# A hybrid decoder step on one core: both halves of every cache page fetched by SyncE, none by GpSimd

## The reference

```python
# cache (DEPTH, N_PHYS, 128, 4, 2, 64): slots k_cmp, v_cmp, k_sel, v_sel; 32 pages per sample
past = cache[layer, page_table, :, :2]                  # every page: compressed keys and values
k_c = _compress(cmp_rows[:, :, 0], w1[0], b1[0], w2[0])
v_c = _compress(cmp_rows[:, :, 1], w1[1], b1[1], w2[1])
o_cmp, imp = _nsa_compressed(q, pos, k_c, v_c)          # imp: weight of each compressed block
idx = _nsa_select(imp, pos, n_blocks)                   # 16 blocks of 64 keys for each query
o_sel = _nsa_sel_attend(q_rot, pos, kg, vg, kpos)       # keys and values of the chosen blocks
o_win = _window_attend(q_rot, ...)                      # the last 512 keys
```

## Time and profile before

| | before |
|---|---|
| median of 3 runs | 2830.82 us |
| profiled execution | 2831.4 us, of which span 2829.7 us |
| mean granted TensorE clock | 0.826 of full speed |
| PE busy | 2296.4 us (81%) |
| DVE / ACT / POOL busy | 1320.5 / 729.9 / 302.0 us |
| fetches of pages | 512 by SyncE, 512 by GpSimd, 128 KB each |

### The profile page before, as it was taken

How to read it: one execution, slowest core, us unless ns; L and a number is a source line. 1 busy time by engine, 2 the same in 40 slices (tenths; PEclk the granted TensorE clock), 3 DMA queues, 4 the chain that set the end, 5 groups by cost and what they waited for, 6 DMA issues and landing times. The chain is left out here.

```text
span 2829.7 us, 35885 instructions
## 1 busy us (share of the span) xinstructions
PE 2296.4 (81%) x12248; PEld 1709.5 (60%) x12248; DVE 1320.5 (47%) x3072; ACT 729.9 (26%) x1512; POOL 302.0 (11%) x516
## 2 busy tenths in 40 slices
PE   6989567569849999997979894774797599999977
PEld 3544467457638887776344443673675488778853
DVE  1343566535515555554114436664454255555431
ACT  1210011024324434341212100110342244434302
POOL 0000000000033222320000000000000332233100
PEclk9999678657879988885989996786587799988869
DMA  4443010010075555642034430100001655566310
GB/s 144 150 141 102 14 28 1 3 44 1 4 172 148 144 142 134 158 114 72 0 107 161 136 89 18 24 1 20 27 1 35 154 144 145 135 158 159 89 67 34
DMA packets 176236, 242.05 MB, mean 86 GB/s; under 512 B 50406, under 2 KB 133126, under 8 KB 175372
## 3 DMA queue, kind: packets, MB, share of 16 engines
q1 hardware_dynamic: 151468, 172.51, 22.1%
q0 software_dynamic: 24576, 67.14, 9.5%
HBM read 223.17 MB, written 24.97 MB: 88 GB/s over the span
## 5 line engine op out<-in xcount | busy, mean ns | idle before, releaser
L588 PE MATMUL bank<-W,hT 128*128 128x512 f32 (+3 forms) x1152 | 444.1, 539 | 30.8 <-DMA W<-in_w_in 21.5
L1526 POOL DMA_DIRECT2D PC<-in_cache_nsa_kv x256 | 150.9, 590 | 2152.0 <-DVEq L195 1687.0
L588 PEld LDWEIGHTS bank<-W,hT 128*128 128x128 f32 x1152 | 216.0, 193 | 228.7 <-issue 182.6
L1212 PE MATMUL bank<-XT,W 128*128 128x256 f32 (+1 forms) x768 | 266.9, 483 | 0.0
L1194 PE MATMUL bank<-CF,RP 128*128 128x128 f32 x1024 | 153.3, 296 | 80.5 <-DVE RP L1182 79.3
L1201 ACT ACTIVATE XT<-bank 128x512 f32<-128x512 f32 x256 | 140.4, 593 | 209.9 <-PE bank L1194 209.0
L1194 PEld LDWEIGHTS bank<-CF,RP 128*128 128x128 f32 x1024 | 123.8, 154 | 94.7 <-DVE RP L1182 84.0
L1694 PE MATMUL bank<-PB,PS 128*128 128x64 f32 x1024 | 176.9, 348 | 3.5 <-ACT PB L1851 3.5
L1526 POOL DMA_DIRECT2D PS<-in_cache_nsa_kv x256 | 150.9, 590 | 220.8 <-issue 165.7
L1694 PEld LDWEIGHTS bank<-PB,PS 128*128 128x128 f32 x1024 | 172.1, 263 | 3.9 <-ACT PB L1851 3.9
L1212 PEld LDWEIGHTS bank<-XT,W 128*128 128x128 f32 x768 | 139.9, 197 | 50.2 <-issue 36.9
(11 more groups left out here) (376 smaller groups left out, 3674.6 us busy)
## 6 DMA issues: line engine op xcount, KB each, us to landing
PC<-in_cache_nsa_kv SPq DMA_DIRECT2D x256, 128.0 KB, 3.8
PC<-in_cache_nsa_kv POOLq DMA_DIRECT2D x256, 128.0 KB, 3.5
PS<-in_cache_nsa_kv POOLq DMA_DIRECT2D x256, 128.0 KB, 4.2
PS<-in_cache_nsa_kv SPq DMA_DIRECT2D x256, 128.0 KB, 4.4
W<-in_w_in SPq DMA_DIRECT2D x48, 512.0 KB, 4.6
XS<-scratch_conv_p SPq DMA_DIRECT2D x24, 384.0 KB
PW<-in_state_nsa_win SPq DMA_DIRECT2D x16, 512.0 KB, 3.9
Wo<-in_w_out SPq DMA_DIRECT2D x4, 2048.0 KB, 12.0
```

What stands on the lines that cost most here:

```text
L588: return nc.tensor.matmul(bk((c * NTILE + t) % 8)[:, 0:b - a], hT[:, k, t * P:(t + 1) * P], W[:, k // 2, k % 2, 0:b - a], start=(k == 0), ...
L1212: mm = nc_(self.v).tensor.matmul(out, self.v['W1'][:, kv, s, :], seg[:, s], start=(s == 0), stop=(s == SEG // PAIRS - 1))
L1526: e.dma_start(where[side * HD:(side + 1) * HD, slot, :, :], A['cache_nsa_kv'][l, page].rearrange("(p r) a g d -> p r (a g d)", r=PAIRS)[:, ...
```

## The change

SyncE now runs the only copy of the sequence and issues both sides of each tile, side 0 and then side 1, behind one wait. GpSimd issues nothing. Each call of `pages` is made twice, once per side. For PC the eight registers of a side are loaded as before; for PS each side has four registers, so a load fetches the four numbers that the next four tiles use. The opening block also issues both sides from SyncE. The data fetched, the buffers and the semaphores are the same, and so is all code of TensorE, ACT and DVE.

```diff
     def pages(e, side, regs, b, n):
-        e.load(regs, ids[0:1, side, b * GT + n:b * GT + n + 8])
+        e.load(regs, ids[0:1, side, b * GT + n:b * GT + n + len(regs)])
         return [e.snap(r) for r in regs]
     def stream(e, side, b, n):
-        for k, page in enumerate(pages(e, side, REGS[side][0:8], b, n)):
+        for k, page in enumerate(pages(e, side, REGS[0][8 * side:8 * side + 8], b, n)):
             fetch(e, PC, k, side, page, 0, pc_rows[side][k])
...
             e.wait_ge(idl, 32)
-            stream(e, 0, 0, 0)
+            for side in range(2):
+                stream(e, side, 0, 0)
             window(e, 0)
...
-        @block.gpsimd
-        def _(e):
-            e.wait_ge(idl, 32)
-            stream(e, 1, 0, 0)
...
-        def transfers(e, side):
-            r = REGS[side]
+        @block.sync
+        def _(e):
+            r = REGS[0]
             def ahead(q, a, z):
...
-                ids_of = pages(e, side, r[0:8], at_q, n)
+                ids_of = [pages(e, side, r[8 * side:8 * side + 8], at_q, n) for side in range(2)]
                 for i in range(a, z):
                     dve.wait(e, f"R{i}.{q}")
-                    fetch(e, PC, i % SLOTS, side, ids_of[i % SLOTS], 0, pc_rows[side][i % SLOTS])
+                    for side in range(2):
+                        fetch(e, PC, i % SLOTS, side, ids_of[side][i % SLOTS], 0, pc_rows[side][i % SLOTS])
             def selected(b, a):
-                ids_of = pages(e, side, r[8:16], b, a // 8 * 8)
+                ids_of = [pages(e, side, r[16 + 4 * side:20 + 4 * side], b, a) for side in range(2)]
                 for k in range(a, a + 4):
-                    fetch(e, PS, k, side, ids_of[k % 8], 256, sel_rows[side][k // 2])
+                    for side in range(2):
+                        fetch(e, PS, k, side, ids_of[side][k - a], 256, sel_rows[side][k // 2])
```

More of the change, by code:

```diff
@@ L1659, in transfers @@
                 if 0 <= p < last:
-                    if side == 0:
-                        pe.wait(e, f"wpv.{p}")
-                        window(e, p + 1)
+                    pe.wait(e, f"wpv.{p}")
+                    window(e, p + 1)
                 if q + 1 < NB:
@@ L1668, in transfers @@
                         selected(p + 1, 4 * k)
[L1670 to L1676, removed]
         @block.tensor
```

## The result

The change makes the kernel slower: the median goes from 2833.25 us (2829.12 to 2840.72, 4 runs) to 2902.8 us (2898.55 to 2911.35, 4 runs). The ratio is 1.0246, 95% interval 1.0213 to 1.0279. The forecast was 2904.5, a ratio of 1.026. I built the same program twice more (experiments 5 and 10) and it gave 1.0183 (1.0116 to 1.025) and 1.019 (1.0144 to 1.0235).

The account below looks back on a forecast made before the run. TensorE was taken to bound most stretches, the DMA engines pass -1. Terms 8 + 26 + 28 + 12 = 74 us on 2831.4 give 2905, or 2904.5 against the median; forecast 2880 to 2930, 80% range 2866 to 2942.

Parts of the forecast that it names:

- Part 1: Opening block, once per layer: US pieces go out later, behind 16 fetches; 8 us in all (bounds 6 to 14).
- Part 2: Pass -1, once per layer: SyncE's row of 44 fetches and its loads makes tile 13 late; 26 us together.
- The sign that I gave for this stretch: Pass -1 in the new profile: DMA share falls from 0.99 to about 0.75, at 131072 bytes per 0.87 us, 150 GB/s.
- Part 3: Twelve steady passes: SyncE's row from R0 to tile 13 takes 44.6 us, longer than every distance available; 28 us.
- The sign of 1 to 5 us more waiting in each pass: Steady passes in the new profile: TensorE's waits on L1194 grow by 1 to 5 us per pass.
- Part 4: Steady passes: new TensorE waits at tile 13 bring falls of the granted clock, 3.5 to 6.5 us each; 12 us taken.
- a border between 2.35 and 3.25: TensorE waits: a fall of the clock follows every 3.25 us wait, but did not follow one of 2.35 us.
- the longer case: Rival, chance 0.2: the clock falls at each new wait and SyncE's row is longer than summed; 2935 to 2953 us.
- only the fill is paid: Rival, chance 0.2: SyncE keeps up in steady passes; opening and pass -1 costs stay; 2865 to 2877 us.
- it isn't slower: Rival, chance 0.03: SyncE alone issues a fetch per 0.61 us, pass -1 stays rate-bound; 2831 us, give or take 8.

Follow-up runs that it names:

- experiment 1: The changed kernel, but GpSimd again issues side 1 of the PS fetches; 2842.98 us, ratio 1.0028 to the kernel before.
- experiment 9: The changed kernel with every load of page numbers split into loads of one register; 3047.75 us, ratio 1.0727 to the kernel before.
- experiment 2: The changed kernel's sequence, with all page fetches and the window issued by GpSimd instead of SyncE; 2866.55 us, ratio 1.0098 to the kernel before.
- experiment 10: The changed kernel, unedited, built a third time; 2901.36 us, ratio 1.019 to the kernel before.
- Experiment 4: The changed kernel, but in the opening block the window and US pieces are issued ahead of side 1's eight fetches; 2885.22 us, ratio 1.0176.
- experiment 11: The kernel before (two queues), with pass -1 reordered to fetch PC tiles ahead of PS pages, and US pieces issued first in the opening; 2784.28 us, ratio 0.9785.
- experiment 3: The changed kernel with page numbers interleaved so that one load serves both sides, half as many loads; 2882.55 us, ratio 1.0162.

## Why the prediction was right, and where it was not

The time was right to 2 us and the main cause is shown: SyncE needs 0.77 to 0.79 us for each fetch, and what it issues in an unbroken row, fetches and loads together, ends too late (experiment 1 shortens the row and parts 2 and 3 vanish; experiment 9 lengthens it and they grow; experiment 2 moves it to a faster issuer and part 3 vanishes). But the sum is better than its terms: two were too high, and places for which I had nothing made up for them. The profiled spans of the three builds of the change were 2900.1, 2891.6 (experiment 5) and 2917.0 us (experiment 10), so being right to 2 us is luck as well. (Its sum is 74 us, which on 2830.8 makes 2904.8; the 2904.5 is 0.3 off.)

**Part 1, the opening: +8 forecast, +8.6 measured.** Right, with its mechanism. The US pieces are issued 6.9 us later within the block (7.0 forecast), and the wait for them is 4.0 us in place of 6.7, where my 4 us per layer stood for 3.7. Experiment 4 takes 7.0 of it back.

**Part 2, pass -1: +26 forecast, +22.1 measured.** The mechanism was right; two sizes were off. The landing is 2.8 us, not 3.3: with GpSimd silent it is below the fastest that before shows in the earlier trace rows. And eight of the ten loads in the row fill four registers, not eight, in 0.30 us. Between the last fetch ahead of a pair of them and the first behind it lie 1.65 us from start to start, so the pair adds 0.87 us, where I took 2 x 0.69 = 1.38. A pair of eight-register loads adds 1.37, as I took. Over the ten loads of the row it is 4 x 0.87 + 1.37 = 4.8 in place of 6.9. With both put right the sum of part 2 is 21 us. I priced a load that the diff shortens from the row of the old one. The sign that I gave for this stretch was wrong too, by its own prices: 0.87 us per fetch has one load in it for eight fetches, where there are two. With two it is 0.96 us and 137 GB/s, and 132 were measured. And the DMA share fell to 0.46, not 0.75. A share of 1 would stand for some 218 GB/s by the row before (216 at 0.99) and for some 290 by the row after (132 at 0.46); the steady stretch shows the same (147 GB/s at 0.60 and at 0.50). So the 0.61 us per fetch that I took as what the DMA engines need is what they took with both engines issuing, and not a price that holds for SyncE alone.

**Part 3, the steady passes: +28 forecast, +12 measured.** By this division, the distances from R0 to the pair sum to 518.8 us over the twelve passes, and were 506.8. The same two prices are the step that failed. By them the row is 44.6 - 0.5 - 2.1 = 42.0 us, and measured to the start of R13 it is 42.6 to 44.5, mean 43.5, since SyncE has hiccups in it (one fetch of 1.01 us in this pass). The mean lateness is only 1.0 us per pass, so an error of 1.1 in a row of 44.6 takes 13 us off the term. Another 3 us go because the pair starts 0.3 us ahead of R13, with the transposes of tile 12, where I let it wait for tile 13. The forecast said that this cover was thin, and had 12 us as its lower end. TensorE's own rows show the waits: ahead of the transposes in the steady passes it is idle for 3.2 us in layer 0 and 6.2 in layer 1, and for nothing before. After, layer 1:

```profile
L1194 PE MATMUL bank<-CF,RP 128*128 128x128 f32 x385 | 57.0, 292 | 6.2 <-DVE RP L1182 6.2
...
L1679 PE MATMUL bank<-sm,ones 128*128 128x64 f32 x36 | 9.3, 354 | 19.5 <-DVE sm L1903 19.5
```

The second row is the wait for the sum of the earlier trace rows, 19.5 us of six passes in before as now. Of the idle time at the transposes only 5.2 us lie ahead of the pairs' first ones; 4.0 lie between tile 12 and tile 13, behind the start of the pair. So some 7 of the 12 us are matmuls ahead of the pair that ran longer. The sign of 1 to 5 us more waiting in each pass came in three passes of twelve (1.8 to 3.6 us); the other nine have 0 to 0.8.

**Part 4, the clock: +12 forecast, and not by the way that I gave.** I priced falls behind new waits of over 3.25 us, and the profile has no such wait. In the steady passes there is one new low stretch, behind the longest of these waits in the trace, 2.92 us, and it is short: from 2517 to 2522 us the granted clock is 0.66, which is some 3.4 us at the lower level.

```profile
2516.34 0.66 PE L1194 MATMUL bank<-CF,RP 128*128 128x128 f32 x4 [2.92 <-DVE RP L1182]
2517.66 0.83 PE L1194 MATMUL bank<-CF,RP 128*128 128x128 f32 x4 [0.66 <-DVE RP L1182]
2518.28 2.76 PE L1212 MATMUL bank<-XT,W 128*128 128x256 f32 x6
```

The six W1 matmuls took 1.56 us at the full clock. What is there instead is more time in the old low stretches of layer 1. Between the pairs of samples 1 and 7, before and after (layer 0, layer 1):

```profile
868.76:1231.49 362.73, 341.23 (x2162) 287.76 (x2161) 197.29 (x474) 145.65 (x234) 109.41 (x186) 0.88 0.58 144
2278.57:2633.75 355.18, 333.51 (x2162) 280.40 (x2161) 197.72 (x474) 145.65 (x234) 109.37 (x186) 0.90 0.60 147
```

```profile
891.47:1259.39 367.92, 343.23 (x2163) 288.22 (x2161) 195.74 (x470) 143.80 (x232) 0.00 (x0) 0.88 0.48 142
2332.05:2703.18 371.13, 343.35 (x2163) 287.66 (x2161) 195.96 (x471) 144.11 (x232) 0.00 (x0) 0.88 0.48 140
```

TensorE is busy for 2.0 us more in layer 0 and 9.8 in layer 1, with the same matmuls and, in layer 1, a clock of 0.88 for 0.90. That is 11.8 of the 21.1 us; the other 9.3 are the idle time above. How much of the 11.8 belongs to the change isn't shown. Before, layer 1 has 7.7 us less of busy time than layer 0, and on two queues, with no late landing, experiment 11 has 678.8 us in both layers together, where before has 674.7, the change 686.6 and its rebuild in experiment 10 677.8. Pass 0 adds 6.3, in layer 0 alone: 29.1 us before and 35.4 after, while layer 1 has 35.4 in both. Either value comes up in either layer over the experiments, by whether a low stretch falls into it; all three builds of the change have 35.4 in both layers. Tail and outside add 12.2, of which 6.7 lie in code that the change doesn't touch; over the eleven experiments the outside varied from 1724.8 to 1743.2. So I can't say how much of these 18.5 us is the change. The forecast's total needs most of them, and to that extent it was lucky.

I also read a row wrongly. The forecast says that the wait of 2.35 us at 2251.88 was not followed by a fall. It was:

```profile
2254.18 1.81 PE L1714 MATMUL bank<-QBD,PS 128*128 128x64 f32 x8
...
2266.94 1.00 PE L1714 MATMUL bank<-QBD,PS 128*128 128x64 f32 x8
```

These eight take 1.81 us behind the wait and 1.00 us when the clock is back. The same wait in layer 0, at 848.36, is the one with no fall behind it (1.00 us for the eight at 850.06). So waits of 2.35 us go both ways, and the argument for a border between 2.35 and 3.25, which I also held against the longer case, had nothing to stand on. I had compared it with the wrong place.

**Waits and clock are not to be added.** Experiment 4 shows why. Here are its two layers, between the same pairs:

```profile
888.03:1257.38 369.35, 338.88 (x2162) 283.10 (x2161) 195.67 (x470) 143.86 (x232) 0.00 (x0) 0.89 0.48 141
2321.99:2694.10 372.11, 333.92 (x2163) 277.67 (x2161) 195.31 (x470) 144.07 (x232) 0.00 (x0) 0.91 0.48 140
```

And TensorE's group of the transposes in its layer 1:

```profile
L1194 PE MATMUL bank<-CF,RP 128*128 128x128 f32 x385 | 56.0, 287 | 16.1 <-DVE RP L1182 16.1
```

In layer 1 TensorE is busy for 9.4 us less than after the change, at a clock of 0.91, and the stretch is still 372.1 us, 1 us longer: the waits ahead of L1194 are 16.1 us and not 6.2. Experiment 10, the change itself, shows it again. Its steady passes take 744.9 us with TensorE busy for only 3.1 us more than before, and the waits ahead of L1194 are 17.4 and 5.9 us. There the longest wait, 4.36 us, was followed by a fall, as forecast (0.57 from 957 to 965 us), and then by a full clock (1.00 from 965 to 980). The steady passes are held by the chain from R0 over SyncE's row to tile 13 and back to R0, and a TensorE that runs faster ahead of the pair comes to it earlier and waits longer. Only where no landing is late does the clock decide a pass. My sum took the price of a fall on top of the lateness, as if both could be paid in the same microsecond.

**The rivals.** That only the fill is paid (2865 to 2877) fell: waits at tile 12 or 13 stand in the steady passes of every build of the change. But its reasons, the fastest landing and cheaper double loads, were both half right, and part 3 came out at the 12 us that it allowed. The longer case (2935 to 2953) fell, as there was one new fall and not six or twelve. That it isn't slower fell with the pitch: 0.77 to 0.79 us with GpSimd silent, and a DMA share of 0.46. The Trainium skill ("DMA: Bandwidth & Descriptors", Issuing engines are not separate DMA queues) calls the time to initiate "usually small relative to the DMA itself"; with 128 KB per fetch here the trace disagrees where many fetches are in flight: 0.78 us on SyncE and 0.64 on GpSimd, against 0.61 at the rate of the earlier trace rows. A single fetch lands 2.8 us after its issue, and beside that the time to initiate is not small either.

**Left open.** The opening's part of the change alone, undone while the rest is kept, wasn't tried; experiment 4 stands in for it. Nor was a row of SyncE's without loads, which by the estimate under experiment 3 would owe nothing in the steady passes. How the clock's share in pass 0, tail and outside divides between the change and chance would need many profiled executions of each kernel.

## What to carry to other kernels

When all transfers of a stage go to one engine, count what that engine needs to issue them from a need to its last landing, loads of addresses included, and compare it with the distance that the consumers leave. The share of the DMA engines doesn't show this limit (0.46 to 0.50 here while the issuer is full). When the difference of two such sums is a few per cent of either, take each price from the form of instruction that the change will run, not from its nearest relative, and count lateness and clock in one chain instead of adding them. And look at the order within the row before moving work between queues: what is asked for ahead of the fetch that is waited for cost more here (45 us of trace) than the second queue had to offer in the same place.

## What the runs showed that I had not expected

A load of page numbers costs by its registers, but with a floor: 0.27 us for one, 0.30 for four, 0.53 for eight, 0.97 for sixteen (medians of experiment 9, of the shorter of the change's loads, of the earlier trace rows and of the longer of experiment 3's).

The fetches land sooner when one engine asks for all: a median of 2.8 us with SyncE alone and also with GpSimd alone (experiment 2), where both queues together had 3.7.

GpSimd's DRAIN at the end of the opening block lasts until its own fetches have landed, 5.76 us in experiment 11, where its last fetch landed 0.4 us before the DRAIN's end, and 6.98 us before. SyncE's took 7 ns there, at 786.9 us, although it had issued the window at 786.24 (landings of it take some 5.7 us). GpSimd's before:

```profile
L195 POOLq DRAIN  x1: 6975/6975/6975, 781.6 to 781.6; - x1
```

So here a prefetch on GpSimd at the end of a block isn't free for the block, and one on SyncE is.
